# Transposes in place of diagonal products in the prompt attention, a later ranking, earlier routes and a ScalarE skip product in a one-launch decoder step

## What is computed

```python
# Mamba branch, 32 heads of 64: the skip product
y = y + d_skip.astype(f32)[:, None] * xs.astype(f32)
# selected and window branch: softmax over keys, then times the values; merged with a gate per head and token
p = jnp.exp(s - m);  p = p / jnp.maximum(jnp.sum(p, axis=-1, keepdims=True), 1e-30)
o = gates[..., 0:1] * o_cmp + gates[..., 1:2] * o_sel + gates[..., 2:3] * o_win
# PEER: 8 heads, each the top 16 of the sums of two top-16 lists
top_s, top_i = lax.top_k(s, PEER_TOPK)
best_s, best_pos = lax.top_k(cand_s, PEER_TOPK)
experts = jnp.take_along_axis(cand_i, best_pos, axis=-1)
g = jax.nn.softmax(best_s, axis=-1)
act = jax.nn.gelu(jnp.einsum('nd,nhkd->nhk', h, peer_u[experts]))
out = jnp.einsum('nhk,nhkd->nd', g * act, peer_v[experts])
```

## Time and profile before

| | |
|---|---|
| median of 3 runs | 2678.91 us (2678.01 to 2681.02) |
| the profiled execution | 2677.47 us, span 2675.6 us |
| busy, share of the span | PE 76%, DVE 55%, POOL 55%, PE weight loads 49%, ACT 23% |
| DMA | 843 MB, mean 315 GB/s |
| group a, conv to query | 8 to 629 us |
| conv b, ssd b, zgate b, bs b | 629, 770, 864, 948 to 1064 us |
| kv b, qk b, cmp b | 1066 to 1181 us |
| attn_prompt | a: 384 to 486 us; b: 1181 to 1360 us |
| sample stages and the rest | 1560 to 2676 us |

### The profile page before, as it was taken

One profiled execution on the slowest core, in us unless ns is written; L12 is line 12 of the kernel. 1 busy time (PEld: TensorE's weight loads), 2 busy tenths in 40 slices (PEclk: granted clock), 3 DMA queues, 4 the chain that ended last, 5 costly groups with the idle time before them and its releaser, 6 DMA issues. The chain is left out here.

```text
span 2675.6 us, 31884 instructions
## 1 busy us (share of the span) xinstructions
PE 2034.1 (76%) x11118; PEld 1309.7 (49%) x11118; DVE 1479.7 (55%) x3747; ACT 624.5 (23%) x1881; POOL 1465.5 (55%) x1488
## 2 busy tenths in 40 slices
PE   8999999988877979989999937855176776655044
PEld 6778876666645657655654713432153442111010
DVE  4331025247999964557621668888876764106900
ACT  5441024224545210024421113321021110000000
POOL 1110000026566864756554787787877777557775
PEclk9999999999987989989999967866589887878577
DMA  5424552546886999989899889999999999999998
GB/s 185 172 80 142 198 181 80 191 164 247 295 319 200 388 390 370 366 319 356 300 343 410 319 292 410 412 404 334 383 393 412 412 410 389 406 385 409 410 409 325
DMA packets 209781, 843.34 MB, mean 315 GB/s; under 512 B 25752, under 2 KB 32728, under 8 KB 190104
## 3 DMA queue, kind: packets, MB, share of 16 engines
q0 software_dynamic: 170912, 644.95, 63.1%
q1 hardware_dynamic: 38712, 196.36, 19.6%
HBM read 821.80 MB, written 23.54 MB: 316 GB/s over the span
## 5 line engine op out<-in xcount | busy, mean ns | idle before, releaser
L3760 POOL DMA_INDIRECT e_ring<-in_peer_u,e_idx x523 | 618.4, 1182 | 294.0 <-issue 134.6
L3924 DVE CUSTOM_DVE_ANT_0 e_ring<-e_ring,e_h 128x1024 f32<-128x1024 f32 x523 | 632.5, 1244 | 61.0 <-DMA e_ring<-in_peer_u,e_idx 40.0
L3760 POOL DMA_INDIRECT e_ring<-in_peer_v,e_idxT x487 | 506.0, 1039 | 257.8 <-issue 135.1
L3827 PE MATMUL ps<-e_ring,e_wz 128*32 128x512 f32 x1948 | 320.4, 704 | 244.9 <-DMA e_ring<-in_peer_v,e_idxT 132.8
L3827 PEld LDWEIGHTS ps<-e_ring,e_wz 128*32 128x32 f32 x1948 | 67.3, 121 | 400.9 <-issue 392.1
L368 PE MATMUL ps<-hT_ahead,wb 128*128 128x320 f32 x384 | 112.0, 448 | 0.0
L2639 POOL DMA_INDIRECT e_ring<-in_cache_cmp_kv,page_rows x8 | 7.8, 976 | 152.4 <-PE ps L2707 151.9
L368 PEld LDWEIGHTS ps<-hT_ahead,wb 128*128 128x128 f32 x384 | 74.2, 198 | 30.2 <-issue 3.6
L3968 DVE TENSOR_TENSOR e_x<-e_x,ps 128x512 f32<-128x512 f32 x10 | 6.4, 684 | 139.4 <-PE ps L3827 139.4
L1229 POOL MEMSET inda<- 128x256 f32 x1 | 0.3, 311 | 148.1 <-POOLq L4238 148.1
L3827 PE MATMUL ps<-ring_pair,e_wz 128*32 128x512 f32 x152 | 65.9, 753 | 17.9 <-DMA e_ring<-in_peer_v,e_idxT 11.3
(11 more groups left out here) (787 smaller groups left out, 4591.9 us busy)
## 6 DMA issues: line engine op xcount, KB each, us to landing
wb<-in_weights SPq DMA_DIRECT2D x65, 1024.0 KB, 7.6
e_ring<-in_weights SPq DMA_DIRECT2D x36, 1024.0 KB, 4.9
wb<-in_late_weights SPq DMA_DIRECT2D x6, 2048.0 KB, 10.6
room<-in_late_weights SPq DMA_DIRECT2D x6, 2048.0 KB, 16.3
h<-in_weights SPq DMA_DIRECT2D x10, 1024.0 KB, 8.6
xs<-in_weights SPq DMA_DIRECT2D x9, 1024.0 KB, 7.9
e_ring<-in_peer_u,e_idx POOLq DMA_INDIRECT x523, 9.1
e_ring<-in_peer_v,e_idxT POOLq DMA_INDIRECT x487, 10.6
```

Source lines behind the costliest of these rows:

```text
L3760: nc.gpsimd.indirect_dma_start(out=self.room(place), out_offset=None, in_=k.peer_u if kind == "u" else k.peer_v, in_offset=off).then_inc(s ...
L3827: last = nc.tensor.matmul(k.ps[32 * b:32 * b + 32, self.SUMS + i, :], self.wz[:, at:at + 32], self.room(self.v_at[n])[:, 512 * i:512 * i + ...
L3924: v.tensor_tensor_reduce(uu, uu, self.h[:, tile % 2, :], 1.0, 0.0, ALU.mult, ALU.add, self.dot[:, tile % 2, t:t + 1]).then_inc(self.dotted, 1)
```

## The change

Four edits. (1) `turn` is a PE transpose against the identity; the scale gate / sum is a [128, 2] product on DVE and is applied by ACT to the weights in SBUF, in place, before the transpose. In group a both copies from PSUM are now on DVE (side 0 was on ACT); in group b both stay on ACT. (2) The ranking of tile 1 begins at place 60 in place of 20. (3) `end_routes` is called ahead of the first conv work of ACT. (4) In ssd of group b the skip product `dx` is made by ACT, eight instructions of 64 columns, in place of one of 512 columns on POOL.

```diff
@@ stage_conv, scalar
                 if f < F:
                     ex.act(f)
+                if f == 0 and not g.first:
+                    k.end_routes()
                 if f == 0:
                     copy_by_head()
...
                 if f == 1 and not g.first:
-                    k.end_routes()
                     for scores_out in k.query_done["scores_out"]:
@@ stage_ssd, gpsimd
-                if u >= 2:
-                    pool.wait_ge(y_half, u - 1)
-                gp.tensor_tensor(v3(dx), x3, by_head(k.dskip_row[:, hs], P), ALU.mult).then_inc(dx_done, 1)
                 if g.first:
+                    if u >= 2:
+                        pool.wait_ge(y_half, u - 1)
+                    gp.tensor_tensor(v3(dx), x3, by_head(k.dskip_row[:, hs], P), ALU.mult).then_inc(dx_done, 1)
@@ stage_ssd, scalar, inputs(u)
+                if u >= 2:
+                    act.wait_ge(y_half, u - 1)
+                for j in range(PER):
+                    hh, at = gr * PER + j, slice(j * HP, j * HP + HP)
+                    last = a.activation(dx[:, u % 2, at], k.xnat[:, c, gr * 512 + j * HP:gr * 512 + j * HP + HP], ACT.Copy,
+                                        scale=k.dskip_row[:, hh:hh + 1])
+                last.then_inc(dx_done, 1)
@@ stage_attn_prompt
-        SIDE_1_ON_ACT = not g.first
+        BY_ACT, BY_DVE = ((), (0, 1)) if g.first else ((0, 1), ())
             def turn(d):
-                pe.wait_ge(exped, 2 * d + 2)
                 for side in range(KVH):
-                    pe.wait_ge(given, 2 * d + side + 1)
+                    pe.wait_ge(scaled, 2 * d + side + 1)
...
-                        last = mm(k.ps[:, 2 + side, kt * P:kt * P + P], weights(2 * d + side)[:, kt * P:kt * P + P],
-                                  diag[:, d % 2, side, :], start=True, stop=True)
+                        last = nc.tensor.transpose(k.ps[:, 2 + side, kt * P:kt * P + P],
+                                                   weights(2 * d + side)[:, kt * P:kt * P + P], k.ident[:])
@@ scalar, at the end of loop i
+                if i < N:
+                    act.wait_ge(given, i + 1)
+                    for u in (2 * i, 2 * i + 1):
+                        w = weights(u)[:, 0:n]
+                        nc.scalar.activation(w, w, ACT.Copy, scale=wgt[:, u:u + 1]).then_inc(scaled, 1)
@@ vector, give(d)
                 own(v.reciprocal(w, ssum[:, 2 * d:2 * d + 2]))
-                if d >= 2:
-                    dve.wait_ge(turned, 2 * d - 2)
-                for side in range(KVH):
-                    c = 3 * (HPK * side + j) + br
-                    v.tensor_scalar(diag[:, d % 2, side, :], k.ident[:], w[:, side:side + 1], k.gates[:, t - t0, c:c + 1],
-                                    ALU.mult, ALU.mult).then_inc(given, 1)
+                v.tensor_tensor(w, w, k.gates[:, t - t0, c:c + 3 * HPK + 1:3 * HPK], ALU.mult).then_inc(given, 1)
@@ Experts
     def rank_place(self, t, step):
         if t == 0 and step >= 0:
-            return 20 + 30 * (step // 9) + step % 9
+            return 60 + 30 * (step // 9) + step % 9
```

More of the change, by code:

```diff
@@ L1552, in stage_attn_prompt @@
         nmax, ssum, wgt = (sb(n, [P, 2 * N]) for n in ("nmax", "ssum", "wgt"))
-        diag = k.mTs[:].rearrange("p f n -> p (f n)").rearrange("p (a s n) -> p a s n", a=2, s=KVH)
-        scored, maxed, exped, given, turned, valued, added, own_s = (
-            sem(n) for n in ("scored", "maxed", "exped", "given", "turned", "valued", "added", "own"))
+        scored, maxed, exped, given, scaled, turned, valued, added, own_s = (
+            sem(n) for n in ("scored", "maxed", "exped", "given", "scaled", "turned", "valued", "added", "own"))
         copied = [sem(f"copied{side}") for side in range(KVH)]
@@ L1712, in _ @@
                 if i:
-                    if i - 1 >= 4:
+                    if BY_ACT and i - 1 >= 4:
                         act.wait_ge(valued, (i - 1) // 2 - 1)
-                    for side in range(KVH if SIDE_1_ON_ACT else 1):
+                    for side in BY_ACT:
                         act.wait_ge(turned, 2 * i - 1 + side)
                         copy(nc.scalar.copy, i - 1, side, copied[side])
+                if i < N:
[3 more added lines that the diff above has]
+                        nc.scalar.activation(w, w, ACT.Copy, scale=wgt[:, u:u + 1]).then_inc(scaled, 1)
             keep_gate(KD - 1)
@@ L1736, in give @@
                 t, br, j = duos[d]
-                w = wgt[:, 2 * d:2 * d + 2]
+                w, c = wgt[:, 2 * d:2 * d + 2], 3 * j + br
                 dve.wait_ge(exped, 2 * d + 2)
                 own(v.reciprocal(w, ssum[:, 2 * d:2 * d + 2]))
-                if d >= 2:
-                    dve.wait_ge(turned, 2 * d - 2)
-                for side in range(KVH):
-                    c = 3 * (HPK * side + j) + br
-                    v.tensor_scalar(diag[:, d % 2, side, :], k.ident[:], w[:, side:side + 1], k.gates[:, t - t0, c:c + 1],
-                                    ALU.mult, ALU.mult).then_inc(given, 1)
+                v.tensor_tensor(w, w, k.gates[:, t - t0, c:c + 3 * HPK + 1:3 * HPK], ALU.mult).then_inc(given, 1)
             def add(n):
@@ L1758, in _ @@
                     ex.dve(i)
-                if i and not SIDE_1_ON_ACT:
-                    dve.wait_ge(turned, 2 * i)
-                    if i - 1 >= 4:
+                if i:
+                    if BY_DVE and i - 1 >= 4:
                         dve.wait_ge(valued, (i - 1) // 2 - 1)
-                    copy(v.tensor_copy, i - 1, 1, copied[1])
+                    for side in BY_DVE:
+                        dve.wait_ge(turned, 2 * i - 1 + side)
+                        copy(v.tensor_copy, i - 1, side, copied[side])
                 if i >= 6 and (i - 6) % 4 == 0:
```

## The result

The changed kernel takes 2666.41 us (median of 20 runs, 2658.07 to 2679.86) where the kernel before takes 2684.86 (20 runs, 2671.78 to 2698.31). The ratio is 0.9929 with a 95% interval of 0.9912 to 0.9947: faster by 0.7%, about 19 us, where 40 were forecast. The profiled execution of the change is one of the slower ones (own time 2674.48, span 2672.7); its stages up to attention b are 20.3 us shorter than before, and 17.5 of them are lost behind it (1306.2 before, 1323.7 after). Second profiles of the two kernels don't repeat that loss (1318.9 and 1320.2); the 1306.2 is the shortest of all thirteen profiles here.

A forecast was written before the change was run, and what follows sets the result against it. PE was taken to bound attention, DVE conv b behind its starting wait, and DMA the tail. The terms −10 − 23 − 17 + 6 + 4 + 0 − 2 − 1 + 3 = −40 gave 2639 us, range 2621 to 2664.

The forecast's parts named there:

- Group a −10, group b −23: Attention: transposes save 0.1375 us a block, less charges for ScalarE's scaling; −10 (−13 to −3) and −23 us (−31 to −8).
- Routes earlier, net −2: Start of conv b: DVE free about 9 us earlier, PE's turns and projection up to 5 later; −2 us (−4 to +3).
- Skip product −1: ssd b: product on ACT relieves DVE by 1.1 us per unit, loads ACT by 2.0; −1 us (−6 to +6).
- Zgate and bs together 0: Zgate b +7 from two heads, bs b −7 with the kv stage; 0 us together (−4 to +4).
- Cmp_prompt +4: cmp_prompt b: two ranking steps of head 6 stand ahead of copies that attention waits for; +4 us (0 to +6).
- Ranking, conv b −17: Conv b: DVE, the bound behind its starting wait, sheds 18 us of ranking; −17 us (−18 to −8).
- head 7 in attention +6: Attention b, tile 2: head 7's ranking bursts of 3 us delay the maximum and Exp; +6 us (0 to +9).
- DMA +3: Attention b: shorter duos would need 401 GB/s, as in the tail, so some transfers come late; +3 us (0 to +6).
- B: Attention and ssd: ScalarE becomes the bound; −20 in all, 2659 us (2652 to 2668); chance 0.20.
- C: Uneven attention duos average out, all 44 us arrive, head 7 and ssd's relief cost nothing; 2618 us (2605 to 2622); chance 0.08.
- D: Ranked names come too late for POOL's gathers; 42 us lost in the DMA-bound part, 2679, no change; chance 0.05.
- E: Attention: transposes don't hold PE's clock, so it runs slower; 2705 us at a share of 0.3; chance 0.05.

The follow-up runs named there:

- e4: The kernel before with the transposes alone, without the other three edits; ratio 0.9892 to the kernel before.
- e8: As e7, but in attention DVE makes a duo's scale ahead of its copies of the duo before; 2630.78 us, ratio 0.9802 to the kernel before.
- e1: The changed kernel with the routes (`end_routes`) back behind block 1 of conv b; ratio 0.990 to the kernel before.
- e3: The changed kernel with the skip product of ssd b back on GpSimd; ratio 0.9912 to the kernel before.
- e2: The changed kernel with the ranking of tile 1 back at place 20; ratio 0.9907 to the kernel before.
- e7: Transposes alone plus tile 1's heads placed by DVE's slack and the routes between blocks 0 and 1 of conv b; ratio 0.9842 to the kernel before.
- e10: The kernel before, unchanged, profiled a second time; 737.3 us from the start of conv b to the end of attention b.

## Why the forecast was off

The measured 2666.41 lies 27 us above the forecast of 2639. Six of them are the base: the forecast stood on 2678.91, the median of three runs, and 20 runs gave 2684.86. The other 21 are, but for about 2 of scatter, in the terms of the sum.

**Transposes: right in sum.** "Group a −10, group b −23" measured −6.3 and, without head 7's ranking, −21.7 to −26.8, so −28 to −33 where −33 was forecast. A turn of eight blocks (the change, tile 3) now takes from 1306.48 to 1307.50:

```profile
1306.48 1.09 PE L1627 MATMUL ps<-ident,apb_p 128*128 128x128 f32 x8
...
1307.50 1.13 PE L1618 MATMUL ps<-kwT,qTb 64*128 64x512 f32 x4
```

That is 0.128 a block, where the forecast took 0.11. TensorE's busy time in turning alone, over 12 duos each of tiles 0, 1 and 3, before and after (window, busy TensorE, weight loads, clock, DMA):

```profile
391.73:424.33 32.60, 8.21 (x49) 6.47 (x48) 1.00 0.33 120
436.61:477.05 40.44, 13.68 (x97) 11.79 (x96) 1.00 0.26 94
1277.42:1344.92 67.50, 24.31 (x193) 22.59 (x192) 1.00 0.86 300
```

```profile
391.08:422.01 30.93, 5.93 (x25) 2.71 (x24) 1.00 0.33 119
433.55:470.46 36.91, 8.54 (x49) 5.03 (x48) 1.00 0.28 101
1268.27:1325.01 56.74, 13.12 (x97) 10.51 (x96) 1.00 0.98 372
```

In tile 3 it fell by 0.117 a block, in tiles 0 and 1 by 0.103 (7.42 us over 72 blocks), and not by 0.1375. The factor in tile 3 is 1.9. That is still further from the four of the Trainium skill ("TensorE: Matmul & The Clock Gate", Terms) than the 2.25 I had from zgate. My reason for discounting, short duos that ScalarE would pace, was largely wrong for group b: TensorE is busy in 56.40 of 56.74 us in tile 3, though ScalarE works 46.14 (0.73 a side for the scaling at 512 columns, 0.67 forecast), and with the transposes alone (e4) TensorE waits 4.2 us for the scaling in all of attention b, where 7.8 were charged. So the sum came out right partly by luck: a saving per block that was put too high and a charge that was too high for group b stood against each other. The four windows of attention after the change, tiles 0, 1, 2 and 3, which answer to the first four of the earlier trace rows (12 duos each, 13 in tile 2):

```profile
391.08:422.01 30.93, 30.25 (x197) 17.09 (x196) 15.78 (x98) 19.40 (x79) 1.87 (x2) 1.00 0.33 119
433.55:470.46 36.91, 35.41 (x236) 19.33 (x236) 22.57 (x101) 24.53 (x79) 1.87 (x2) 1.00 0.28 101
1187.82:1248.99 61.17, 57.63 (x337) 29.27 (x337) 50.11 (x160) 42.05 (x116) 42.68 (x40) 0.97 0.95 344
1268.27:1325.01 56.74, 56.40 (x358) 28.83 (x357) 40.55 (x112) 46.14 (x107) 39.63 (x38) 1.00 0.98 372
```

In group a the hand-off did cost: not ScalarE's load but DVE's order. At 0.103 a block 9.9 us were to be had there; the change got 6.3 of them and e8 9.2.

**"Routes earlier, net −2" is the step that failed most.** It measured +5.8 (e1), outside its bounds of −4 to +3. I had seen up to 5 us of TensorE's delay (its turns came 4.5 later), and booked against them a gain for DVE that needs block 1 as well as block 0; block 1 came late by the same wait, and TensorE's work behind the wait ran at a lower granted clock, for which the sum had no term.

**"Skip product −1" measured +3.8** (e3), inside its bounds of −6 to +6. The relief of DVE was sized at 9 us from one stretched dot product; DVE's busy time fell by 2.4. The term in ScalarE's chain was real.

**"Zgate and bs together 0"** measured +5.3 between the two kernels and +6.3 by e2: I let a gain of 7 in bs b pay for a loss of 7 in zgate b. The wait in bs b for the first merge fell from 12.15 to 4.8, but that stage is only 0.5 us shorter. TensorE's busy time in it rose from 101.83 to 103.90 and its wait for a gather of `peer_v` from 2.0 to 5.6, at a DMA share of 0.98 before and 0.97 after; whether the DMA sets the length of that stage was not tried. In zgate b three ranking steps now end two places ahead of the weights that TensorE waits for (5.01 before, 10.81 now).

**"Cmp_prompt +4"** measured +4.6 to +7.8 by which profile of before it is held against, 6.2 by e2. **"Ranking, conv b −17"** measured −9.3 in conv b itself and −15.7 with ssd b, whose first unit waits for the last convolution (e2); **head 7 in attention +6** measured +5.6. These were right. **"DMA +3"** was not taken apart from the rest by any run. The saving up to attention b does reach the end in e4 (29.1 in the stages; 29 by the ratio, 18 to 40) and in e8 (53.3; 53, 47 to 59), while in e7 52.1 stand against 42 (35 to 50); such a term can't be told from this scatter.

Put together from the runs: −6.3 − 26.8 + 5.6 + 6.2 − 15.7 + 6.3 + 5.8 + 3.8 = −21, against −20.3 in the stages and −19 by the ratio (with e10 for the kernel before, −16 against −17.9). So the forecast's path was right in its two large terms, and four small ones, each with the wrong sign or too small, ate half of it. All three edits beside the transposes together cost 8.8 us, or 12.7 if conv b of the transposes alone is taken as the 141.3 of the kernel before.

**Rivals.** B's number is the nearest: −20 from its terms, and 2666.41 inside its 2652 to 2668. That is luck for the whole, for its largest term, group b −14 because ScalarE becomes the bound, is refuted (−21.7 to −26.8); but its −6 for group a and its +6 for ssd, where ScalarE's instructions lie in the chain of the units, are what came (−6.3, +3.8). C's uneven duos largely averaged out in group b, but 28 to 33 of its 44 us came, and neither ssd nor head 7 came for nothing. D did not come: no wait of GpSimd for the copied names shows in the change's list of waits, and its wait for DVE's dots between 620 and 1350 us is 137.0 against 130.6 before. (The forecast said that `index_head` keeps its places; it moves by 40 with the ranking, from 50 + 30h to 90 + 30h.) E did not come either: the clock of the four stretches of attention, a fifth to a quarter of whose busy TensorE time is transposes (5.93, 8.54, 11.61 and 13.12 us), is 1.00, 1.00, 0.97 and 1.00. The rule of the Trainium skill ("TensorE: Matmul & The Clock Gate", Part 4: PE-mode transpose), that transposes don't count as busy in the same way, is not tested by that, since the rest of TensorE's work runs in the same stretches; no run here has transposes alone.

## What to carry to other kernels

Before an instruction that waits is moved ahead on an in-order engine, list everything that it is moved past and who waits for that; a few lines later in the same queue (e7) turned a loss of 5.8 us into a gain of 4.8 to 6.5. Background work is to be placed stage by stage where its engine has slack and away from the places where another engine waits for a result of the same queue; here a uniform shift mostly moved the loss (e2). Where single runs scatter by nearly 1%, compare stage lengths between two profiles, and take a second profile of the same kernel to see what repeats.

## What the runs showed of the hardware

A transpose of 128x128 beside real loads took 0.128 us a block in attention, 0.11 in the short pair in zgate. A ScalarE product in SBUF took 394 ns at 128 columns, 500 at 256, 614 at 384 and 725 at 512, as much as the Exp of the same width (389, 494, 605, 716), not as little as a copy from PSUM (588 at 512). After a wait of 4.35 us two projections took 10.92 us in place of 8.88. And one stage with unchanged code took 141.2, 141.3 or 145.2 us by the clock that it was granted.
